# A hybrid decoder layer with a grouped MoE: phase tables made in an earlier stage, and expert rows added into one buffer by indirect writes

## The reference: one layer for 1024 prompt tokens and 8 sample tokens

```python
h = modulate(rms_norm(x))                       # adaLN
q, k, v, z, beta, alpha, u = split(h @ w_in)    # q, k, v through a short conv
o_a = gdn_chunked(q, k, v, g, beta, state)      # gated DeltaNet, 4 heads of 128
y   = s5_scan(u, ...)                           # 32 groups, 64 complex states each
o_b = rms_norm(gelu(y) * sigmoid(gelu(y) @ glu_w + glu_b))
x   = x + gate1 * (concat(o_a, o_b) @ w_out)
t   = modulate(rms_norm(x))
# MoE: 16 experts in 4 groups, the best group, then its 2 best experts
wts = take(scores, idx); wts = wts / sum(wts)
act = silu(t @ w_gate[e]) * (t @ w_up[e]) * combine[:, e]
out = sum_e act @ w_down[e]
y   = rms_norm(x + gate2 * out) * final_g
```

## Time and profile before

| | |
|---|---|
| time, median of 3 (lowest, highest) | 1297.97 us (1297.96, 1301.45) |
| profiled execution: its own time, its span | 1301.65 us, 1300.0 us |
| TensorE clock granted, mean | 0.929 of full speed |
| instructions | 15152 |
| PE, DVE, ACT, POOL busy | 1118.5 (86%), 548.8 (42%), 306.0 (24%), 231.9 us (18%) |
| MB moved by DMA | 173.49 |

### The profile page before, as it was taken

One profiled execution on the slowest core, in us unless ns is written; L12 is line 12 of the kernel. 1 busy time (PEld: TensorE's weight loads), 2 busy tenths in 40 slices (PEclk: granted clock), 3 DMA queues, 4 the chain that ended last, 5 costly groups with the idle time before them and its releaser, 6 DMA issues. The chain is left out here.

```text
span 1300.0 us, 15152 instructions
## 1 busy us (share of the span) xinstructions
PE 1118.5 (86%) x5094; PEld 675.3 (52%) x5095; DVE 548.8 (42%) x1234; ACT 306.0 (24%) x684; POOL 231.9 (18%) x364
## 2 busy tenths in 40 slices
PE   4899998999976997667869799996499999889876
PEld 4466665447756776465654445543244444444332
DVE  4153344414365356888942433545411111111128
ACT  5121112342125233122214323232011111101033
POOL 0100000003323241544440000102311111101050
PEclk8999999999989989688879899997699999999887
DMA  9557091000132002434417100006378565798373
GB/s 349 167 205 259 6 290 65 1 1 9 30 68 65 2 2 74 136 133 139 139 23 294 66 17 33 32 33 149 105 259 257 166 219 170 246 323 289 110 276 131
DMA packets 124704, 173.49 MB, mean 133 GB/s; under 512 B 36430, under 2 KB 80195, under 8 KB 124639
## 3 DMA queue, kind: packets, MB, share of 16 engines
q1 hardware_dynamic: 113644, 138.51, 32.7%
q0 software_dynamic: 7376, 21.59, 5.0%
q10 hardware_dynamic: 3626, 12.64, 2.4%
HBM read 127.40 MB, written 44.24 MB: 132 GB/s over the span
## 5 line engine op out<-in xcount | busy, mean ns | idle before, releaser
L2066 PE MATMUL bank<-w_out,H 128*128 x384 | 171.9, 601 | 10.0 <-DMA w_out<-in_w_up 5.2
L350 PE MATMUL bank<-hT,w_ring 128*128 128x344 f32 x576 | 169.5, 456 | 3.8 <-ACT hT L533 3.8
L350 PEld LDWEIGHTS bank<-hT,w_ring 128*128 128x128 f32 x576 | 110.0, 192 | 62.2 <-issue 5.2
L2066 PEld LDWEIGHTS bank<-w_out,H 128*128 128x128 f32 x384 | 72.3, 192 | 107.0 <-issue 107.0
L2346 PE MATMUL bank<-w_out,hT 128*128 128x512 f32 (+1 forms) x288 | 127.5, 595 | 0.5 <-DVE hT L1858 0.5
L435 PE MATMUL bank<-w_ring,hT 128*128 128x512 f32 x256 | 114.7, 605 | 3.6 <-DVE ZO L766 3.6
L2130 DVE TENSOR_TENSOR H<-H,bank 128x256 f32<-128x256 f32 x24 | 10.1, 421 | 245.4 <-ACT H L2101 245.4
L2050 PE MATMUL bank<-y1T,H 128*128 x192 | 91.3, 619 | 10.7 <-DVE H L2139 7.9
L435 PEld LDWEIGHTS bank<-w_ring,hT 128*128 128x128 f32 x256 | 64.2, 254 | 49.5 <-issue 32.1
L2346 PEld LDWEIGHTS bank<-w_out,hT 128*128 128x128 f32 (+1 forms) x288 | 50.1, 179 | 64.5 <-issue 63.7
L2050 PEld LDWEIGHTS bank<-y1T,H 128*128 128x128 f32 x192 | 35.4, 194 | 52.3 <-issue 52.3
(11 more groups left out here) (518 smaller groups left out, 1836.2 us busy)
## 6 DMA issues: line engine op xcount, KB each, us to landing
ys_d<-ZO SPq DMA_DIRECT2D x18, 1024.0 KB, 13.4
y1T<-in_w_down SPq DMA_DIRECT2D x16, 1024.0 KB, 5.6
w_out<-in_w_gate SPq DMA_DIRECT2D x16, 1024.0 KB
w_out<-in_w_up SPq DMA_DIRECT2D x16, 1024.0 KB
ys_d<-H ACTq DMA_DIRECT2D x24, 512.0 KB, 5.6
w_ring<-in_w_in SPq DMA_DIRECT2D x4, 2048.0 KB, 8.7
y1T<-in_w_ada SPq DMA_DIRECT2D x4, 2048.0 KB, 8.2
hT<-in_w_ada SPq DMA_DIRECT2D x4, 2048.0 KB, 13.1
```

Of the source, the lines that this page charges most:

```text
L350: mm = t.matmul(ps[3 * (m % 2) + s][:, 0:SEG], w_ring[:, q % 2, k, (m % 4) * P:(m % 4 + 1) * P], hT[:, k, s * SEG:(s + 1) * SEG], start=(k ...
L2066: mm = t.matmul(ps[2 + p][:, :], xT[p][:, k, :], wgu[:, bass.ds(buf, 1), k, :].rearrange("p o n -> p (o n)"), start=(k == 0), stop=(k == K ...
```

## The change

It has five parts.

1. The eight phase tables (cosine and sine of four quarters) are made in stage s2, DVE the cosines and POOL the sines, in the room of V and of `crow_room`; SP stores them to a DRAM buffer `e_d` (eight stores of 128 x 1032), and s4 loads them back, two quarters ahead of its other loads and the others as buffers come free. Since ACT's sums of squares go to `crow_room` too, ACT waits for all eight stores at b = 8. For this S5's constants are made earlier: their DMAs go out at the second weight load, and the rates, powers and inputs stand between the pieces of the conv.
2. `ys_d` (18 blocks of zeros of 1 MB) gives way to `acc_d` (1160 rows in token order, ten stores of zeros), and `h2_d` gets 128 more rows of zeros.
3. The id lists are two wide: the token's id and its router weight. Free places of a list point at row T of `h2_d` and `acc_d` with weight 0. `choose(r)` works out the weights of its round in 8 more small DVE operations and reductions; the DVE work behind `slots` that made positions and weights is gone.
4. In the MoE loop ACT's two copies of down scale each row by its weight, and POOL writes the slot's rows into `acc_d` by an indirect DMA that adds to what stands there, waits for its end, and only then frees the buffer, since two slots can add to the same row. POOL's own program of a slot grows from a list and a gather to: put (of two slots before), keep (a copy of the list), list, gather.
5. At the end SP loads 9 tiles of `acc_d` straight; the 18 gathers, the diagonals and the products of PE are gone. Gate2's rows are made ahead of the loop.

The diff, cut to what the steps below speak of:

```diff
+        e_d, e_out = dram("e_d", (4, 2, P, NE)), [sem("e_out0"), sem("e_out1")]
...
+                def zero_rows():
+                    zeros = Z[:, NT, :].unsqueeze(1).to_broadcast([P, 2, 512])
+                    for dst in [acc_d[i * P:min((i + 1) * P, TP), :] for i in range(NT + 2)] + [h2_d[T:TP, :]]:
...
+                for q in range(4):
+                    dve.wait(sp, f"e{q}_7")
+                    sp.dma_start(e_d[q, 0], Es_(q, 0)).then_inc(e_out[q % 2], 16)
+                    pool.wait(sp, f"e{q}_7")
+                    sp.dma_start(e_d[q, 1], Es_(q, 1)).then_inc(e_out[q % 2], 16)
...
                         pe.wait(a, "pick7")
+                        a.wait_ge(e_out[0], 64)
+                        a.wait_ge(e_out[1], 64)
...
+                def tables(q):
+                    gs, Ec, Es = slice(q * NG, (q + 1) * NG), phase(q, 0), phase(q, 1)
+                    if q >= 2:
+                        v.wait_ge(e_out[q % 2], 32)
+                    dve.did(v.memset(Ec[:, :, 0:1], 1.0))
+                    dve.did(v.tensor_copy(Ec[:, :, 1:2], ph[:, 0, gs].unsqueeze(2)), f"e{q}_0")
+                    wd = 1
+                    while wd < NCH:
+                        step = wd.bit_length()
+                        pool.wait(v, f"e{q}_{step - 1}")
+                        cw, sw = (x[:, :, wd:wd + 1].to_broadcast([P, NG, wd]) for x in (Ec, Es))
+                        tt(e1[:, :, 0:wd], Ec[:, :, 1:wd + 1], cw, ALU.mult)
+                        tt(e2[:, :, 0:wd], Es[:, :, 1:wd + 1], sw, ALU.mult, wait=False)
+                        tt(Ec[:, :, wd + 1:2 * wd + 1], e1[:, :, 0:wd], e2[:, :, 0:wd], ALU.subtract, f"e{q}_{step}")
+                        wd *= 2
...
+                    if m == 5:
+                        rates()
+                    elif m == 8:
+                        first_power()
+                    elif m == 9:
+                        inputs()
+                    elif m == 10:
+                        powers(2, 6)
+                    elif m == 11:
+                        powers(6, LAGS + 1)
+                pe.wait(v, "gate_rows")
+                for x in range(3):
+                    dve.did(v.tensor_copy(gate_rows[:, x * SEG:(x + 1) * SEG], ps[x][:, 0:SEG]), "gate_rows")
+                power_copies()
+                eighth_angle()
...
+                tables(0)
+                tables(1)
+                tables(2)
+                tables(3)
                 act.wait(v, "ln")
...
+        def load_phases(sp, q):
+            for n, tab in enumerate((Ec2, Es2)):
+                sp.dma_start(tab[:, q % 2].rearrange("p g n -> p (g n)"), e_d[q, n]).then_inc(e_land[q % 2], 16)
...
+                for c in range(2):
+                    load_phases(sp, c)
                 for c in range(2):
                     load_ada(sp, c)
...
+                    if q in (1, 2):
+                        dve.wait(sp, f"zc{q - 1}")
+                        pool.wait(sp, f"zl{q - 1}")
+                        load_phases(sp, q + 1)
...
-                    if q >= 2:
-                        dve.wait(g, f"zc{q - 2}")
-                    pool.drain(g)
-                    pool.did(g.tensor_copy(Es[:, :, 1:2], ph[:, 1, q * NG:(q + 1) * NG].unsqueeze(2)), f"e{q}_0")
...
-                phases(0)
...
+                    g.wait_ge(e_land[q % 2], 32 * (q // 2 + 1))
...
-                    if q < 3:
-                        phases(q + 1)
...
-                    if q >= 2:
-                        pool.wait(v, f"zl{q - 2}")
-                    dve.did(v.tensor_copy(Ec[:, :, 1:2], ph[:, 0, gs].unsqueeze(2)), f"e{q}_0")
...
-                    pool.wait(v, f"e{q}_7")
+                    v.wait_ge(e_land[q % 2], 32 * (q // 2 + 1))
...
-            def load(it, p):
-                g.wait_ge(who_in[p], it * 16 + 16)
+            def gather(n, p):
+                g.wait_ge(who_in[p], n * 16 + 16)
                 g.sem_inc(listed, 1)
                 g.wait_ge(scat, 16 * 18)
                 g.indirect_dma_start(xin[p][:, :], None, h2_d, bass.IndirectOffsetOnAxis(ap=who[p][:, 0:1], axis=0)).then_inc(x_in[p], 16)
 
+            def keep(n, p, s):
+                g.wait_ge(x_in[p], n * 16 + 16)
+                g.sem_inc(listed, 1)
+                g.wait_ge(scat, 16 * 18)
+                g.tensor_copy(kept_i[p], who[p]).then_inc(kept, 1)
+                g.wait_ge(kept, s + 1)
+            def put(n, p, s):
+                g.wait_ge(y_half, s + 1)
+                g.wait_ge(y_sb, s + 1)
+                g.sem_inc(listed, 1)
+                g.wait_ge(scat, 16 * 18)
+                g.indirect_dma_start(acc_d, bass.IndirectOffsetOnAxis(ap=kept_i[p][:, 0:1], axis=0), yo[p][:, :], None,
+                                     compute_op=ALU.add).then_inc(y_out[p], 16)
+                g.wait_ge(y_out[p], n * 16 + 16)
+                g.sem_inc(y_free[p], 1)
             def body(it):
-                if isinstance(it, int):
-                    load(0, 1)
-                else:
-                    g.wait_ge(xT_ps, it * 2)
-                    load(it, 1)
-                g.wait_ge(xT_ps, it * 2 + 1)
-                list_in(it * 2 + 2, 0)
-                load(it + 1, 0)
-                g.wait_ge(x_in[1], it * 16 + 16)
-                list_in(it * 2 + 3, 1)
+                for p in range(2):
+                    s = it * 2 + p
+                    if not isinstance(it, int):
+                        put(it - 1, p, s - 2)
+                    keep(it, p, s)
+                    list_in(s + 2, p)
+                    g.wait_ge(xT_ps, s + 1)
+                    gather(it + 1, p)
+            def tail(it, s):
+                put(it, 0, s - 1)
+                put(it, 1, s)
+                g.sem_inc(y_done, 1)
...
                 a.wait_ge(dn_ps, s + 1)
                 if not (isinstance(it, int) and it == 0):
-                    a.wait_ge(y_out[p], it * 16)
-                a.activation(yo[p][:, 0:512], ps[5][:, :], ACT.Copy).then_inc(y_half, 1)
-                a.activation(yo[p][:, 512:D], ps[6][:, :], ACT.Copy).then_inc(y_sb, 1)
-                a.wait_ge(y_half, s + 1)
-                a.wait_ge(y_sb, s + 1)
-                a.dma_start(ys_v[bass.ds(s, 1)].rearrange("o p d -> (o p) d"), yo[p][:, :]).then_inc(y_out[p], 16)
+                    a.wait_ge(y_free[p], it + 1)
+                a.wait_ge(kept, s + 1)
+                weight = kept_f[p][:, 1:2]
+                a.activation(yo[p][:, 0:512], ps[5][:, :], ACT.Identity, scale=weight).then_inc(y_half, 1)
+                a.activation(yo[p][:, 512:D], ps[6][:, :], ACT.Identity, scale=weight).then_inc(y_sb, 1)
...
+            sp.wait_ge(y_done, 1)
+            for i in range(9):
+                n = P if i < NT else DEC
+                sp.dma_start(ya[i][0:n, :], acc_d[i * P:i * P + n, :]).then_inc(ygot[i], 16)
...
-                    fpe.wait(v, f"mix{i}")
-                    for half_ in range(2):
-                        c = slice(half_ * 512, (half_ + 1) * 512)
-                        fdve.did(v.tensor_tensor(mix[:, c], ps[(5, 2)[i % 2] + half_][0:n, :], gt[0:n, c], ALU.mult), f"g{i}")
+                    v.wait_ge(ygot[i], 16)
+                    fdve.did(v.tensor_tensor(mix, ya[i][0:n, :], gt[0:n, :], ALU.mult), f"g{i}")
...
+                    for j, oh in enumerate((one, two)):
+                        tt(m_, oh, lg[:, lo:hi, :], ALU.mult)
+                        dve.drain(v)
+                        dve.did(v.tensor_reduce(col[:, 2 + j, lo:hi], m_, AX.X, ALU.add))
+                    tt(col[:, 4, lo:hi], col[:, 2, lo:hi], col[:, 3, lo:hi], ALU.add)
+                    dve.drain(v)
+                    dve.did(v.reciprocal(col[:, 4, lo:hi], col[:, 4, lo:hi]))
+                    dve.drain(v)
+                    for j in range(2):
+                        dve.did(v.tensor_tensor(pairs_f[:, 2 * lo + j:2 * hi:2, 1], col[:, 2 + j, lo:hi], col[:, 4, lo:hi], ALU.mult))
```

421 lines of the change are left out of this document (191 added, 230 removed).

## The result

The changed kernel takes 1344.64 us, the median of 4 runs (1340.34 to 1348.06), against 1298.49 of the kernel before (1297.96 to 1301.45): 1.034 times as long, 95% interval 1.031 to 1.037. The forecast was 1280. The profiled execution took 1341.66 us.

A forecast was written before the change was run, and what follows sets the result against it. PE was taken to bound s2's start and the MoE loop, DVE the stretch 523 to 675 us. +16.6 - 35.4 + 1.2 + 12 - 12.5 = -18.1 from 1301.65: 1283.5, or 1280 against the median 1297.97; 8 in 10: 1263 to 1310.

The forecast's parts named there:

- Stage s2, +16.6: Making and storing the tables in s2 delays ACT's squares' copies and PE: +16.6 us, bounds +14.6 to +20.
- Stage s4, -35.4: Without making tables in s4, DVE's turns start earlier, 8.8 us in three quarters, 8.9 in the first: -35.4, bounds -26 to -47.
- what is late next is PE's last product of b: In s4, DVE's turn then waits only for that product, at 611.3, so it starts 8.8 us earlier, not 12.9.
- rival C: PE and its 0.80 clock bound s4's quarters, saving 26 us: 1289; chance within the 0.46 shared with the main forecast.
- Routing, +1.2: Eight more small DVE operations in each routing round, half of each exposed: +1.2 us, bounds 0 to +3.5.
- The loop, +12: MoE loop: POOL's longer chain exceeds PE's 12.2 us slot in eight slots, less some cover: +12 us, bounds +3 to +90.
- L: Issue and landing of the adding write in the MoE loop: 8.0 us where weights are loading, 5.0 where they aren't.
- Eight slots each 2.0 over: MoE loop: the last eight slots beside weight loads overrun by 2.0 us each; earlier six have spare slots between.
- Rival B: MoE loop: the adding write sets the slot, each us above 6.0 costing 22 us; at L = 8, 1312 us; chance 0.23.
- loop at +5 to +20: The main forecast's range for the MoE loop, taken with rival C: 1272 to 1290 us, likeliest 1280; chance 0.46.
- B': MoE loop: the add costs the whole landing twice, L = 11.2 us, 17.4 for a slot: 1382 us; chance 0.05.
- The end, -12.5: After the loop: DVE starts 7.3 us sooner and its own loop is 5.2 shorter: -12.5, bounds -6 to -16.

The follow-up runs named there:

- e7: e6 with powers 6 to 8 put back behind the copies of the gate rows, where the kernel before had them: 1272.81 us, 0.979 of the kernel before.
- e3: The changed kernel with the adding left out of the indirect write, all waits kept: 1310.88 us, 1.010 of the kernel before.
- e10: e2 with the adding left out of the indirect write: 1286.63 us, 0.989 of the kernel before.
- e2: The changed kernel with POOL's wait for the write's end behind the next gather and the next list asked for ahead of the write: 1290.68 us, ratio 0.994.
- e1: The kernel before with only the early phase tables and S5 constants (s2 and s4); lists, loop and end as before: 1297.42 us, ratio 0.999.
- e6: e2 with the first two phase tables moved ahead of the gates' first sum on DVE: 1282.26 us, 0.985 of the kernel before.
- e5: The changed kernel with only the next list asked for ahead of the adding write, the wait still before the gather: 1297.98 us, ratio 1.000.
- e4: The changed kernel with PE's three register loads for the down product moved ahead of the transposes: 1346.12 us, 1.034 of the kernel before.

## Why the prediction was wrong

**Stage s2, +16.6: right** in size and in the place that ends the wait. The tables ran 51.2 instead of 52.4, and the stage was 16.3 later. (From 311.2 the shift is 15.8, not the 15.6 of the sum.) What it left out is that, with the constants made earlier, DVE is idle for 22.6 us ahead of absx; e7 shows that with half of the tables there, and the three powers back behind the gate rows, the stage costs 0.3.

**Stage s4, -35.4: too large**, -25.1 in the trace. The first quarter gave 9.1 (13.0 from the first b to the turn before, 3.9 now; 8.9 predicted). The other three gave 7.1, 6.1 and 5.8, not 8.8, and 3 came back behind the last turn: the step "what is late next is PE's last product of b" looked at one turn only. With the table away, PE's products and DVE's turn form one loop, in which PE waits 4.4 for DVE and DVE 2 to 4 for PE. This is rival C's saving of 26, by a wait between the two engines; that PE's clock bound the quarters, which C names as well, is not shown (0.80 before from 523 to 675 us, 0.85 now).

**Routing, +1.2: right**, 0.6.

**The loop, +12: wrong, +60.8.** The form of the sum was right, and its two sides weren't. L was put at 8.0 beside weight loads and at 5.0 elsewhere. The trace has 1.6 + 138.9 / 22 = 7.9 on the mean, but not as that mixture: 9.8 to 10.7 in six slots and 6.5 to 7.7 in 16. So both values were about 2 too low, and that the mean lies at the higher of them is chance. What is left of POOL's chain was put at 6.2 (its terms as printed make 6.1) and is 1.4 (table load) + 0.6 + 3.4 (the list) + 0.99 + 0.3 + 0.2 = 6.9, so the chain takes 14.7 on the mean. Against 12.2 that is 2.5 in each of 22 slots, 55 of the 60.8 us.

The step that failed is "Eight slots each 2.0 over": it let the other slots run below 12.2 and took spare time from them, on L = 5.0, which is the plain store's 2.6, the lowest of 24 and of a transfer that reads no destination, plus 2.4 for the issue and the read. The plain indirect write of e3 lands in 3.3 at best, the adding one in 6.2. The 0.6 in it for the longer issue had no row behind it; it measured 1617 against 984 ns, which is as much. With the measured terms no slot's chain is below 12.2 (the shortest is 12.2), and no spare is left to pay with. What was not seen at all: that PE's order puts the transposes ahead of the down product, so that a late gather delays the very write that the next but one gather stands behind, and that PE then pays for its register loads (22.0) and runs down at a lower clock (108.2 us for 192 products instead of 91.3).

**Rival B** had the mechanism and, at L = 8, 1312; measured at L = 7.9 it was 1344.6. Its formula counts L alone, and lacks the 0.7 of the chain (15 us) and the lower saving of s4 (10). Its chance of 0.23 was small beside the 0.46 for a loop at +5 to +20: the two nearest rows of the trace both had no add in them.

**The doubling that the Trainium skill would have given** ("Collectives: The Full Stack", on the bandwidth ceiling): the whole landing does not double here, so B' did not come. Between e3 and the changed kernel it goes from 5.2 to 6.9 us at the median, 1.3 times, and from 3.3 to 6.2 at best, 1.9 times; between e10 and e2 from 4.1 to 6.4, 1.6 times, and from 3.3 to 6.1, 1.8 times.

**The end, -12.5: right**, -11.2; 3.8 of it for the start instead of 7.3, 7.4 for the loop of DVE instead of 5.2. The last write can't start before the one ahead of it has landed: 1291.19 instead of 1288.6. From its start to DVE's first product it is 10.2 us; the sum had 9.3, of which the 3.8 for the first load had no row behind it.

## What to carry to other kernels

A wait for the end of one's own transfer holds back everything that stands behind it in the same engine's program: put next to the issue it made this kernel 3.4% slower, put behind the next gather, with the list ahead of the write and the same transfers, 0.6% faster than the one before. When a stage has an engine with little to spare, add up its chain for the fast case too: if even that is as long as the stage's period (12.2 us here), each of the slots pays, and not only those with traffic. And work that is moved early wants to stand where its engine is idle, not just before the wait that it delays: the same tables and powers cost the stage 16 us as placed, and 0.3 when half of the tables stood ahead of the gates' first sum and three powers behind the gate rows; that version, with the wait behind, takes 1272.8 us, 2.1% less than before.

## What the runs showed of the hardware that was not expected

The same instructions of stage s3 took 180.7 or 180.8 us in three of these traces and 184 to 186 in eight others (182.2 in that of before). A stretch of 30 us at the same distance from the stage's start, in the changed kernel and in e1 (length, busy time and number of PE's products, then of the weight loads and the other engines, granted clock, share of the DMA engines, GB/s):

```profile
459.60:489.60 30.00, 26.72 (x302) 21.43 (x300) 16.04 (x53) 13.64 (x52) 13.34 (x23) 0.94 0.01 1
```

```profile
459.80:489.80 30.00, 26.99 (x278) 21.31 (x276) 16.13 (x53) 13.28 (x53) 14.14 (x25) 0.83 0.01 1
```

The first has a mean granted clock of 0.94 and 302 products, the second 0.83 and 278, at about the same busy time: the busy time does not show the difference, the count does. The clock of this stretch is not the whole of it: at 0.88 to 0.89 e2, e6 and e10 have 269 or 270 there. What in the kernel or the chip decides how long a run takes for the stage is open. The times of whole executions go with the clock too: of the ten of e5, five took 1291.8 to 1296.0 us at a mean granted clock of 0.918 to 0.920, and five 1300.0 to 1307.7 at 0.911 to 0.915. So a stage's difference of a few us between two single traces says little.

PE's down product in the loop takes 3.70 us at a granted clock of 1.00, in 14 of the 24 slots of the changed kernel and in 23 before. In the other ten it takes 5.16 to 6.37, at 0.57 to 0.71 on the mean; ahead of each PE had been idle for its register loads, and in nine of the ten for a gather before that. One of each (columns as above):

```profile
1103.06:1108.45 5.39, 5.39 (x9) 2.37 (x10) 0.00 (x0) 0.00 (x0) 1.57 (x3) 0.68 0.01 0
1116.67:1120.37 3.70, 3.70 (x8) 1.43 (x8) 1.16 (x2) 0.00 (x0) 0.78 (x2) 1.00 0.00 0
```

The first had 1.49 us of idle time ahead of its transposes and 2.50 behind them. So part of what a late gather costs is paid at the lower clock, behind it: 16.9 us over the loop.

The register loads from SBUF on PE's sequencer (three of them ahead of each down product) left PE idle in one place and for 2.8 us before, where products were queued, and for 22.0 us in twelve places once the transposes had come late; moved ahead of the transposes, in e4, they left none.
